# Transposes of attention values and outputs: TensorE's 128x128 against VectorE's 32x32 with placement by DMA

## What is computed

```python
mod = silu(c) @ ada_w + ada_b
shift, scale, gate = split(mod, 3)
h = rms_norm(x, norm_pre) * (1 + scale) + shift
q, k, v, z = the four slices of h @ w_in       # 2048 columns each
# per head: sc[m] = q[m] @ k[m].T * 128**-0.5, masked by chunks of 64
attn = softmax(sc[0]) - lam * softmax(sc[1])
o = attn @ v
o = rms_norm(o, subln_g) * (1 - lambda_init)   # over the 256 columns of a head
y = (o * silu(z)) @ w_out
out = x + gate * rms_norm(y, norm_post)
```

## Time and profile before

| | |
|---|---|
| median of 3 runs | 1907.58 us (1907.35 to 1908.47) |
| profiled execution, its own time | 1907.34 us |
| span of the profiled execution | 1905.5 us |
| busy: PE, PE's weight loads | 1866.0, 1540.9 us |
| busy: VectorE, ScalarE, POOL | 1379.5, 810.1, 794.4 us |
| instructions: PE, VectorE, ScalarE, POOL | 9072, 2028, 1516, 844 |
| packets and data of the DMA engines | 394048, 473.16 MB |

### The profile page before, as it was taken

One profiled execution on the slowest core, in us unless ns is written; L12 is line 12 of the kernel. 1 busy time (PEld: TensorE's weight loads), 2 busy tenths in 40 slices (PEclk: granted clock), 3 DMA queues, 4 the chain that ended last, 5 costly groups with the idle time before them and its releaser, 6 DMA issues.

```text
span 1905.5 us, 26384 instructions
## 1 busy us (share of the span) xinstructions
PE 1866.0 (98%) x9072; PEld 1540.9 (81%) x9072; DVE 1379.5 (72%) x2028; ACT 810.1 (43%) x1516; POOL 794.4 (42%) x844
## 2 busy tenths in 40 slices
PE   4999999999999999999999999999999999999998
PEld 1488888888888888888888888888888888888886
DVE  3687888886655546787887877878778776569467
ACT  5633333333444433444443444444444445546452
POOL 2076565655644523344344434434443422116023
PEclk9999999999999999999999999999999999999999
DMA  9898898886674698786877778686777679657777
GB/s 354 253 313 279 274 297 278 284 290 232 214 267 160 237 356 263 225 250 192 253 229 227 235 216 252 198 254 212 232 240 221 213 228 291 207 186 257 258 240 265
DMA packets 394048, 473.16 MB, mean 248 GB/s; under 512 B 22614, under 2 KB 268476, under 8 KB 391228
## 3 DMA queue, kind: packets, MB, share of 16 engines
q1 hardware_dynamic: 393632, 471.43, 76.4%
q10 hardware_dynamic: 284, 0.05, 0.0%
HBM read 323.54 MB, written 147.86 MB: 247 GB/s over the span
## 4 chain that ended last, share of the span: by engine, by line
PE 93%; DVE 1%; DMA 1%; ACT 0%; issue 0%; SPq 0%; POOL 0%; DVEq 0%; POOLq 0%; ACTq 0%
PE ps L1752 30%; PE ps L1754 30%; PE ps L1753 30%; PE ps L1885 2%; PE ps L1861 1%; PE ps L1904 1%; PE ps L1721 0%; DMA ubf<-s_dr 0%; DMA z_dr<-cc 0%; PE ps L1833 0%; DVE ring L1310 0%; ACT h L1040 0%; DVE xt L1632 0%; DVE tB L1330 0%; DVE tB L1327 0%
## 5 line engine op out<-in xcount | busy, mean ns | idle before, releaser
L1752 PE MATMUL ps<-blk,ring 128*128 128x512 f32 x1524 | 603.3, 396 | 2.6 <-DVE blk L1357 1.9
L1754 PE MATMUL ps<-blk,ring 128*128 128x512 f32 x1524 | 594.6, 390 | 0.0
L1753 PE MATMUL ps<-blk,ring 128*128 128x512 f32 x1524 | 594.2, 390 | 0.0
L1752 PEld LDWEIGHTS ps<-blk,ring 128*128 128x128 f32 x1524 | 286.3, 188 | 66.0 <-issue 9.7
L1754 PEld LDWEIGHTS ps<-blk,ring 128*128 128x128 f32 x1524 | 286.0, 188 | 60.8
L1753 PEld LDWEIGHTS ps<-blk,ring 128*128 128x128 f32 x1524 | 286.5, 188 | 55.8
L1310 DVE TENSOR_TENSOR ring<-sums,ring 128x512 fp32r<-128x512 f32 x256 | 234.7, 917 | 95.5 <-ACT ring L1006 93.6
L836 POOL TENSOR_TENSOR sums<-raw 128x512 f32<-128x512 f32 x128 | 191.5, 1496 | 226.9 <-DVE ring L1310 206.0
L1006 ACT ACTIVATE ring<-sums 128x512 fp32r<-128x512 f32 x256 | 160.6, 628 | 179.3 <-PE ps L1754 175.6
L1310 DVE TENSOR_TENSOR ring<-raw,ring 128x512 fp32r<-128x512 f32 x192 | 179.2, 934 | 58.9 <-ACT ring L1006 58.5
L836 POOL TENSOR_TENSOR sums<-sums,raw 128x512 f32<-128x512 f32 x128 | 190.2, 1486 | 20.8 <-DVE ring L1310 14.3
(11 more groups left out here) (159 smaller groups left out, 3181.7 us busy)
## 6 DMA issues: line engine op xcount, KB each, us to landing
raw<-in_diff_w_in_dram SPq DMA_DIRECT2D x64, 1024.0 KB, 7.8
d_dr<-cc SPq DMA_DIRECT2D x124, 256.0 KB, 3.2
cc<-d_dr SPq DMA_DIRECT2D x124, 256.0 KB, 4.1
ubf<-s_dr SPq DMA_DIRECT2D x113, 256.0 KB, 5.0
ada<-in_ada_w_dram SPq DMA_DIRECT2D x88, 256.0 KB, 7.3
tb<-in_diff_w_out_dram SPq DMA_DIRECT2D x32, 512.0 KB, 5.5
t_dr<-tb SPq DMA_DIRECT2D x32, 512.0 KB, 4.9
ada<-in_ada_w_dram SPq DMA_DIRECT2D x32, 512.0 KB
```

The costliest lines, as they stand in the source:

```text
L1752: MM(dst, a_hi, b_hi, start=start, stop=False, skip_group_check=True)
L1753: MM(dst, a_hi, b_lo, start=False, stop=False, skip_group_check=True)
L1754: return MM(dst, a_lo, b_hi, start=False, stop=stop, skip_group_check=True)
```

## The change

The value blocks are turned by VectorE, straight after the product that completes them, each in one instruction that turns every square of 32x32 in its place. Stores write the tile as it lies (2 KB a partition), and `load_v` places the squares, in four transfers of 32 partitions with runs of 32 floats. `v_turn` is gone from PE, and the parts and stores of a value block come one product after it (no `lag`). Outputs are scaled and multiplied by the sub-norm's weights in one instruction, with the weights as a row on all partitions. Then VectorE turns the squares into PSUM, and the gate is one multiplication with a z that `load_z` brings in the same arrangement (four transfers). `ozf` and `osum` become one tile, which `store_pair` stores after the sums, in four transfers that place the squares. The diff leaves out the semaphores' renaming and one count of them at the start.

```diff
+SIDE = 32
...
-        sub8 = at("sub8", [P, 2], F32)
...
-        ozf = at("ozf", [P, 2, 2, P], F32, z_at)
-        osum = at("osum", [P, 4, P], F32, z_at)
+        o_all = at("o_all", [P, 8, P], F32, z_at)
+        ozf, osum = o_all[:, 0:4].rearrange("p (t m) n -> p t m n", t=2), o_all[:, 4:8]
...
+        sub_row = at("sub_row", [P, VD], F32, z_at)
...
-        v_dr = dram("v_dr", [HEADS * SEQ, 2, VD])
+        v_dr = dram("v_dr", [HEADS * 2, 2, 2, P, HALF])
...
-        s_dr = dram("s_dr", [8, HEADS, P, PAIRS, P])
+        s_dr = dram("s_dr", [HEADS, 8 * P, PAIRS, P])
...
+        PAIR_STORED = 16 * (P // SIDE)
...
-        def lag(n):
-            return 2 if head_part(n // NP)[1] == 2 else 1
...
                     if part == 2:
-                        dst = v_dr[h * SEQ + half * HALF:h * SEQ + (half + 1) * HALF].rearrange("(t p) s d -> p t s d", p=P)
-                        sp.dma_start(dst[:, :, s, m * P:(m + 1) * P],
-                                     src.rearrange("p (t d) -> p t d", t=HT).bitcast(F32)).then_inc(stored[o], 16)
+                        sp.dma_start(v_dr[h * 2 + half, s, m], src.bitcast(F32)).then_inc(stored[o], 16)
...
-                sp.dma_start(v_sb[:, qb].bitcast(F32),
-                             v_dr[h * SEQ + qb * P:h * SEQ + (qb + 1) * P]).then_inc(v_ld[qb % 2], 16)
+                for c in range(0, P, SIDE):
+                    n = qb % HT * P + c
+                    sp.dma_start(v_sb[c:c + SIDE, qb].rearrange("i s (c j) -> i (s c) j", j=SIDE).bitcast(F32),
+                                 v_dr[h * 2 + qb // HT, :, :, :, n:n + SIDE].rearrange(
+                                     "s m (c i) j -> i (s m c) j", i=SIDE)).then_inc(v_ld[qb % 2], 16)
...
-                sp.dma_start(z_sb[:, :, :],
-                             z_dr[h * 2:h * 2 + 2, :, qb * P:(qb + 1) * P].rearrange("m p n -> p m n")).then_inc(z_ld, 16)
+                for c in range(0, P, SIDE):
+                    sp.dma_start(z_sb[c:c + SIDE].rearrange("j m (b i) -> j (m b) i", i=SIDE),
+                                 z_dr[h * 2:h * 2 + 2, :, qb * P + c:qb * P + c + SIDE].rearrange(
+                                     "m (b j) i -> j (m b) i", j=SIDE)).then_inc(z_ld, 16)
...
                 sp.wait_ge(ozf_ok, h * NB + 2 * p + 2)
-                sp.dma_start(s_dr[0:4, h, :, p].rearrange("o p n -> p o n"),
-                             ozf.rearrange("p i m n -> p (i m) n")).then_inc(s_st, 16)
                 sp.wait_ge(osum_ok, 4 * (h * PAIRS + p + 1))
-                sp.dma_start(s_dr[4:8, h, :, p].rearrange("o p n -> p o n"), osum[:, :, :]).then_inc(s_st, 16)
+                for c in range(0, P, SIDE):
+                    sp.dma_start(s_dr[h, :, p, c:c + SIDE].rearrange("(o j) i -> j o i", j=SIDE),
+                                 o_all[c:c + SIDE].rearrange("j o (b i) -> j (o b) i", i=SIDE)).then_inc(s_st, 16)
...
+                if n == NA + 12:
+                    sp.dma_start(sub_row[:, :], subln[None, :].to_broadcast([P, VD])).then_inc(sub_in, 16)
...
+                if n % NP in BLOCK and head_part(n // NP)[1] == 2:
+                    v_turn(n)
...
+            def v_turn(n):
+                i, pi = divmod(n, NP)
+                h, o = head_part(i)[0], AT[pi]
+                if h or o:
+                    dve.wait_ge(post_d, 12 * h + o if o else 12 * (h - 1) + 4)
+                dve.wait_ge(ev_d, 3 * GP + NP * (i - GP) + pi + 1)
+                V.transpose(ps[:, VX], cc[:, buffer_of(i, BLOCK[pi])]).then_inc(vt_ok, 1)
...
-                V.tensor_scalar(o_sb[:, :], ps[:, OB, 0:VD], ofac[:, 0:1], None, ALU.mult).then_inc(o_ok, 1)
+                else:
+                    dve.wait_ge(cols_ok, 2)
+                STT(o_sb[:, :], ps[:, OB, 0:VD], ofac[:, 0:1], sub_row[:, :], ALU.mult, ALU.mult).then_inc(o_ok, 1)
...
-                dve.wait_ge(z_ld, (a + 1) * 16)
-                if a > 1:
-                    dve.wait_ge(s_st, 32 * (a // 2))
-                for m in range(2):
-                    i = STT(ozf[:, a % 2, m], ps[:, OB, VD + m * P:VD + (m + 1) * P], sub8[:, m:m + 1],
-                            z_sb[:, m], ALU.mult, ALU.mult)
-                i.then_inc(ozf_ok, 1)
+                dve.wait_ge(o_ok, a + 1)
+                V.transpose(ps[:, OB, VD:2 * VD], o_sb[:, :]).then_inc(oT_done, 1)
+                dve.wait_ge(z_ld, (a + 1) * 16 * (P // SIDE))
+                if a > 1:
+                    dve.wait_ge(s_st, PAIR_STORED * (a // 2))
+                dve.wait_ge(oT_done, a + 1)
+                TTV(ozf[:, a % 2], ps[:, OB, VD:2 * VD].rearrange("p (m n) -> p m n", m=2), z_sb[:, :, :],
+                    ALU.mult).then_inc(ozf_ok, 1)
...
+            V.tensor_scalar(sub_row[:, :], sub_row[:, :], (1.0 - LAMBDA_INIT) / 2, None, ALU.mult).then_inc(cols_ok, 1)
...
-            def v_turn(i, pi):
-                h, _ = head_part(i)
-                b, o = BLOCK[pi], AT[pi]
-                pe.wait_ge(*read_out(i, pi))
-                if h or o:
-                    pe.wait_ge(post_d, 12 * h + o if o else 12 * (h - 1) + 4)
-                for t in range(HT):
-                    last = TR(ps[:, VX, t * P:(t + 1) * P], cc[:, buffer_of(i, b), t * P:(t + 1) * P], ident[:, :])
-                last.then_inc(vt_mm, 1)
...
-                pe.wait_ge(v_ld[qb % 2], (a // 2 + 1) * 16)
+                pe.wait_ge(v_ld[qb % 2], (a // 2 + 1) * 16 * (P // SIDE))
...
-            def o_turn(h, qb):
-                a = h * NB + qb
-                pe.wait_ge(o_ok, a + 1)
-                for m in range(2):
-                    last = TR(ps[:, OB, VD + m * P:VD + (m + 1) * P], o_sb[:, m * P:(m + 1) * P], ident[:, :])
-                last.then_inc(oT_done, 1)
```

More of the change, by code:

```diff
@@ L680, in slot @@
                 for w in (n - 3, n - 2):
-                    if w >= NA and w % NP in BLOCK and w == n - 1 - lag(w):
+                    if w >= NA and w % NP in BLOCK and w == n - 2:
                         store(*divmod(w, NP))
                 for w in (n - 5, n - 4):
-                    if w >= NA and w % NP in BLOCK and w == n - 3 - lag(w):
+                    if w >= NA and w % NP in BLOCK and w == n - 4:
                         f, b = w // NP, BLOCK[w % NP]
@@ L726, in _ @@
                     load_qk(*divmod(a + 1, NB))
-                    for _ in range(sum(SPREAD[qb])):
+                    for k in range(sum(SPREAD[qb])):
                         slot(n)
@@ L1009, in _ @@
             act.wait_ge(c_in, 16)
-            A(cexp[:, :], craw[:, :], ACT.Exp, scale=-1.0).then_inc(c_e, 1)
+            A(cexp[:, :], craw[:, :], ACT.Exp, scale=-1.0).then_inc(c_ok, 1)
             for t in range(TT):
@@ L1124, in post_high @@
                 if part == 2:
-                    act.wait_ge(vt_mm, 4 * h + o + 1)
+                    act.wait_ge(vt_ok, 4 * h + o + 1)
                     A(ev[:, o], ps[:, VX], ACT.Copy).then_inc(post_hi, 1)
@@ L1141, in posts @@
                 for w in (n - 2, n - 1):
-                    if w >= NA and w % NP in BLOCK and w == n - lag(w):
+                    if w >= NA and w % NP in BLOCK and w == n - 1:
                         post_high(w)
@@ L1282, in _ @@
             V.memset(yss[:, :, :, :], D * EPS).then_inc(yss_c, 1)
-            dve.wait_ge(c_e, 1)
+            dve.wait_ge(c_ok, 2)
             V.tensor_scalar(cexp[:, :], cexp[:, :], 1.0, None, ALU.add).then_inc(c_ok, 1)
-            dve.wait_ge(c_ok, 2)
+            dve.wait_ge(c_ok, 3)
             V.reciprocal(cexp[:, :], cexp[:, :]).then_inc(c_ok, 1)
-            dve.wait_ge(c_ok, 3)
+            dve.wait_ge(c_ok, 4)
             TTV(cact[:, :], craw[:, :], cexp[:, :], ALU.mult).then_inc(c_ok, 1)
@@ L1557, in _ @@
                 take(n)
+            dve.wait_ge(sub_in, 16)
+            V.tensor_scalar(sub_row[:, :], sub_row[:, :], (1.0 - LAMBDA_INIT) / 2, None, ALU.mult).then_inc(cols_ok, 1)
             n = NA + PARTS_IN * NP
@@ L1727, in ada_rows @@
                 if s == 0:
-                    pe.wait_ge(c_ok, 4)
+                    pe.wait_ge(c_ok, 5)
                 pe.wait_ge(*ada_landed(s))
@@ L1844, in slot @@
             def slot(n, js=range(KB)):
-                if js.start == 0 and n - 2 >= NA and (n - 2) % NP in BLOCK:
-                    f, fp = divmod(n - 2, NP)
-                    h, part = head_part(f)
-                    if part == 2:
-                        v_turn(f, fp)
                 if n < NALL:
                     product(n, js)
-            def v_turn(i, pi):
-                h, _ = head_part(i)
-                b, o = BLOCK[pi], AT[pi]
-                pe.wait_ge(*read_out(i, pi))
-                if h or o:
-                    pe.wait_ge(post_d, 12 * h + o if o else 12 * (h - 1) + 4)
-                for t in range(HT):
-                    last = TR(ps[:, VX, t * P:(t + 1) * P], cc[:, buffer_of(i, b), t * P:(t + 1) * P], ident[:, :])
-                last.then_inc(vt_mm, 1)
             def scores(h, qb, m):
@@ L1898, in weighted @@
```

(12 more changed lines are left out.)

9 lines of the change are left out of this document (4 added, 5 removed).

## The result

The changed kernel takes 1944.06 us (median of 4 runs, 1941.61 to 1945.62) against 1907.46 of the kernel before on the same chip: a ratio of 1.0188, 95% interval 1.0175 to 1.0200. The forecast was 1883, faster. The profiled execution took 1941.61 us, its span is 1939.7. It took between 1906.98 and 1907.63 us on all the chips used, so the medians of two experiments may be subtracted to about half a microsecond.

The account below looks back on a forecast made before the run. The prediction took PE, busy for 98% of the span, to bound the kernel: 1907.3 - 28.0 (transposes off PE) + 3.5 (queues) = 1882.8, said as 1883, own range 1876 to 1893, 8 in 10 from 1875 to 1960.

Parts of the forecast that it names:

- What goes from PE: PE loses 128 transposes of values and 128 of outputs, 14.0 us each, 28.0 us in all, all on the path.
- What comes to DVE: VectorE's turns at 686 and 410 ns, less the gate's saving, add 31 us net, costed at nothing apart from queues meeting.
- the cover: VectorE's idle time, 107.5 us waiting for scores and 45 us for products between 720 and 1640 us, hides its new work.
- rival 1: VectorE waits for z or ACT, PE for VectorE before the weighted sums: 15 to 25 us lost, 1895 to 1905; chance 0.13.
- What comes to SP: SyncE's queue gets 56 more issues a head at 0.45 us; 65 of 107 us leave it open.
- 4.5 us to spare: In the block after a pair store, the values land near 932, ahead of PE's need at 936.67.
- rival 2: Short packets cost a flat price, from 21.6 ns up, delaying the values' load after a pair store: 1928 or 2355; chance 0.31.
- What comes to the DMA engines: Packets a head grow by 30720; at 9.6 ns per 128 B packet, engines need 76 us of 107 and keep up.
- The sum: Whole kernel: 1907.3 - 28.0 + 3.5 = 1882.8, said as 1883, own range 1876 to 1893; chance 0.50.
- where queues meet: An allowance of 0.5 us a head, 3.5 us over seven heads, the only cost added to the forecast.

Follow-up runs that it names:

- one long DMA each: Changed kernel with values' load, z load and pair store each as one DMA of long runs, squares not placed: 1903.11 us, ratio 0.9979.
- four long DMAs each: Changed kernel with values' load, z load and pair store each as four DMAs of long runs, squares not placed: 1907.88 us, ratio 1.0002.
- one short DMA each: Changed kernel with values' load, z load and pair store each as one DMA of 128 B runs, squares not placed: 1914.32 us, ratio 1.0041.
- changed, pair store long: Changed kernel with the pair store as one DMA of 512 B runs, squares of the outputs not placed: 1912.21 us, ratio 1.0027.
- the outputs alone: Changed kernel with the values' part undone: only outputs go by VectorE and squares, values turned by PE as before: 1942.59 us, ratio 1.0178.
- the values' half alone: Changed kernel with the outputs' part undone: only values go by VectorE and squares, outputs turned by PE as before: 1905.67 us, ratio 0.9990.

## Why the prediction was wrong, step by step

**What goes from PE: right, and 4 us too high.** 28.0 us were forecast, and the kernel without turns and with long transfers shows 24.

**What comes to DVE: the durations nearly right, the cover wrong.** The turns of 512 and 256 columns took 727 and 442 ns (686 and 410 taken), the gate 425; the gate gave back 11 us instead of 17, since two gates' records had overlapped (38.4 us busy, not 128 x 340 ns = 43.5), so the net is 40 us, not 31. But "so I cost this at nothing" failed: the turns cost 19.7 us. The step read the cover from the head as a whole, idle time of 107.5 and 45 us over seven heads. It isn't spread evenly: in the value part's blocks the chain leaves PE for 25 us and follows mostly DVE's fixed order. The text had that (10.29 of 12.4 us in one block) and used it for rival 1 alone. Rival 1 named this mechanism (1895 to 1905) and the 1903 of the long transfers is inside it.

**What comes to SP: this is the step that turned the sign.** "65 of 107 us leave the queue open" had the count right (144 issues a head; 145 in the trace) and the price wrong: 0.58 us each, not 0.45, makes 84 us of 113.5. The gaps of 0.04 us between two issues and the waits for its own stores (106 us over 900, 13 a head) come on top, and only about 8 us a head are left in which the queue waits for another engine; before it was 60. The values' load has no 4.5 us to spare: its last issue ended at 1052.5, 7.6 us after the z loads began, and the data landed another 3.1 us later. The price was read from single issues of long runs, and for long runs it holds even in a crowd. The table gives the seven heads of five traces (means a head, us):

| kernel | issues | one issue | issuing in all | the queue's waits | a head | behind the heads |
|---|---|---|---|---|---|---|
| one long DMA each | 85 | 0.47 | 40 | 66 | 110.2 | 342.1 |
| four long DMAs each | 145 | 0.48 | 69 | 34 | 110.2 | 348.3 |
| one short DMA each | 85 | 0.77 | 65 | 42 | 111.0 | 348.2 |
| changed, pair store long | 133 | 0.54 | 72 | 32 | 110.3 | 349.9 |
| the whole change | 145 | 0.58 | 84 | 23 | 113.5 | 356.7 |

Short runs raise the price, the number multiplies it, and the heads grow only when the queue has little waiting left. In full, the heads grow by 3.3 us each over one long DMA, 23 in all. That the sum is the queue's and not one transfer's is borne out by the values' load issued earlier (nothing gained) and by z issued elsewhere (17 us gained).

**What comes behind the heads: no term at all.** The sum has nothing for the last head's stage, and rival 2 gave it room. It takes 12.7 us more than before, and at least 6 us more than with one long DMA each in all four kernels below it in the table. The chain of this stage holds 42.5 us of SyncE's queue (2.7 before), over a third of them at the loads of the output product's units (L711, L717), which stand in the same queue.

**What comes to the DMA engines: the price right, the sum low.** 9.6 ns a packet of 128 B were taken. A full microsecond after (1190.6 to 1191.6: page of packets, then its window) has

```profile
DMA packets 1664, 0.21 MB, mean 210 GB/s; under 512 B 1664, under 2 KB 1664, under 8 KB 1664
...
1190.60:1191.60 1.00, 1.00 (x6) 0.84 (x5) 1.00 (x2) 0.53 (x1) 1.00 (x1) 1.00 1.35 210
```

16 / 1664 = 9.6 ns. But the sum of a head was low from the start: 1073 us of engine by the prediction's prices, 1314 in the trace before (a share of 0.75 and not 0.61). After, it is 1551, a share of 0.85, where 1221 and 0.71 were forecast; with the prediction's own count, -245 + 40960 p = 237, p is 11.8 ns. All this is far from the 21.6 at which rival 2 decides. The sign is rival 2's, and what was to show it is there in part (PE waits for the values' load, issues of up to 2.8 us, heads of over 110 us), but its mechanism is not: the engines have room, at a share of 0.85, and with 0.88 in the kernel of one short DMA each a head takes 111.0 us. That 1944 lies in the wide range (1875 to 1960) is luck: the range reaches there for rival 2. The Trainium skill ("DMA: Bandwidth & Descriptors", Specifications) wants at least 512 B for the full rate, and the trace agrees: 210 GB/s in this microsecond against 342 with packets of 512 B. What the prediction read from it, that a short packet costs what one of 512 B does, is not so here: 9.6 ns against 23.9.

**The sum.** From 1883.4, the kernel with neither turns nor short transfers: +19.7 for the turns on DVE, +4.8 for four issues instead of one, +11.2 for short runs, +25 for both at once, gives 1944.1. The 25 is what remains, so the sum closes by itself; that a full queue makes it is argued from the table, the clock's part is in it, and the share of each was not measured. The forecast had -28.0 + 3.5: the 3.5, the half microsecond a head "where queues meet", is the term that failed. From 1883.4 it measured 60.6, of which 19.7 from DVE's turns and 41 from the transfers.

## What to carry to other kernels

A queue that issues DMAs is an engine: give it a busy share with the price per issue taken from transfers with runs as short as the new ones, count its waits for its own stores, and look whether it still waits for the others. Once it hardly does, a late transfer is someone's stall; the one reordering tried here only changed whose. An average with room is not enough either, as the outputs alone show: look at the order within the tightest block, and at the last stage. Idle time covers new work only in the blocks where that work lands, so read the cover there, not over the period. And split a change that moves work on two paths before judging it: the values' half alone costs nothing (0.999), but gains nothing either; no complete kernel here is clearly faster than the one before.

## What the runs showed of the hardware that was not expected

The time that an issue holds its queue grows with short runs: a median of 468 ns for one long load of values, 958 ns for the same bytes in 128 B runs, up to 4.8 us; on ScalarE's queue up to 4.65 us, in which ScalarE computes nothing. It does not grow with the number of issues alone (0.47 us for 85 a head, 0.48 for 145). Packets of 128 B took 9.6 ns each in a full microsecond, those of 512 B 23.9. After a wait of PE of 2.5 us the granted clock fell to 0.60 for four us in one trace and stayed at 1.00 in another; after one of 4.9 us it was 0.50 for four. A transpose of 32x32 squares on VectorE costs little more than a two-operand instruction of that size (727 to 686 ns at 512 columns), from SBUF into PSUM. An instruction of VectorE on two SBUF operands of 256 columns took 484 ns on average before and 1341 after; of two looked at, the long one started just behind one of GpSimd's sums and the short one beside none. And moving 27 us of work from VectorE to GpSimd left VectorE as busy as before.
